# Late modulation rows: the sum over a partition's eight weights moved from TensorE to GpSimd, half of the pieces in the channel stage

## What is computed

```python
c_act = jax.nn.silu(c)                                # 1 x 1024
mod = c_act @ w_ada[l] + b_ada[l]                     # 1 x 6144
sh1, sc1, g1, sh2, sc2, g2 = jnp.split(mod, 6, axis=-1)
u = layernorm(x) * (1 + sc1) + sh1
y = mixer(u, ...)          # mLSTM heads and latent attention heads
x = post_ln(alpha * x + (1 + g1) * y)
u = layernorm(x) * (1 + sc2) + sh2
y = hier_moe(u, ...)
x = post_ln(alpha * x + (1 + g2) * y)

# mLSTM part of the mixer, for each direction, over chunks of 128 tokens
w = exp(d_log - m_t)
s = (q @ k.T) * w
h = (a * (q @ C) + s @ v) / max(|den|, exp(-m_t))
C = decay * C + (k * wg).T @ v
```

## Time and profile before

| what | us |
|---|---|
| three runs: median, lowest, highest | 1534.51, 1533.08, 1534.63 |
| the profiled execution's own time | 1535.46 |
| its span, first to last instruction | 1533.5 |
| TensorE busy | 1487.1 (97%) |
| VectorE busy | 565.2 (37%) |
| ScalarE busy | 357.5 (23%) |
| GpSimd busy | 97.5 (6%) |

### The profile page before, as it was taken

How to read it: one execution, slowest core, us unless ns; L and a number is a source line. 1 busy time by engine, 2 the same in 40 slices (tenths; PEclk the granted TensorE clock), 3 DMA queues, 4 the chain that set the end, 5 groups by cost and what they waited for, 6 DMA issues and landing times. The chain is left out here.

```text
span 1533.5 us, 19984 instructions
## 1 busy us (share of the span) xinstructions
PE 1487.1 (97%) x7403; PEld 818.7 (53%) x7404; DVE 565.2 (37%) x1134; ACT 357.5 (23%) x738; POOL 97.5 (6%) x97
## 2 busy tenths in 40 slices
PE   7999999999989999999999899999999999999997
PEld 4555554447868666674555554444444444444443
DVE  2222126567769433334867711111011011011118
ACT  1122122137624344352111010110111111111111
POOL 0000002000000000000000011111111111111110
PEclk9999999999999999999999899999999999999999
DMA  9401011128730200004111589869789879999965
GB/s 343 159 28 41 0 8 31 41 69 248 248 114 2 110 0 0 0 0 154 76 56 55 192 344 391 370 243 415 317 327 425 314 314 414 423 385 399 425 282 208
DMA packets 101798, 305.51 MB, mean 199 GB/s; under 512 B 18353, under 2 KB 61661, under 8 KB 92536
## 3 DMA queue, kind: packets, MB, share of 16 engines
q1 hardware_dynamic: 93064, 287.08, 48.6%
q0 software_dynamic: 8064, 16.80, 3.0%
q10 hardware_dynamic: 624, 1.03, 0.2%
HBM read 289.86 MB, written 25.76 MB: 206 GB/s over the span
## 5 line engine op out<-in xcount | busy, mean ns | idle before, releaser
L1908 PE MATMUL ps<-w_down_sb,hidT 128*128 x320 | 153.4, 612 | 0.0
L457 PE MATMUL ps<-w_in_tok,uT 128*128 128x512 f32 (+2 forms) x384 | 141.5, 529 | 0.0
L1892 PE MATMUL ps<-w_gate_sb,x_slotsT 128*128 x320 | 140.7, 593 | 0.7 <-ACT x_slotsT L1991 0.7
L1892 PE MATMUL ps<-w_up_sb,x_slotsT 128*128 x320 | 140.6, 592 | 0.0
L1563 PE MATMUL ps<-uT,hT 128*128 128x512 f32 x256 | 112.8, 594 | 0.0
L624 PE MATMUL ps<-uT,mod 128*128 128x512 f32 x256 | 111.0, 594 | 0.8 <-PEq L213 0.8
L2145 DVE TENSOR_TENSOR hid<-silu_g,ps 128x512 f32<-128x512 f32 x20 | 13.8, 688 | 258.0 <-PE ps L1892 258.0
L457 PEld LDWEIGHTS ps<-w_in_tok,uT 128*128 128x128 f32 x384 | 72.7, 190 | 65.3 <-issue 43.9
L1892 PEld LDWEIGHTS ps<-w_gate_sb,x_slotsT 128*128 128x128 f32 x320 | 60.8, 190 | 76.8 <-issue 76.8
L1892 PEld LDWEIGHTS ps<-w_up_sb,x_slotsT 128*128 128x128 f32 x320 | 60.9, 190 | 76.5 <-issue 76.5
L1908 PEld LDWEIGHTS ps<-w_down_sb,hidT 128*128 128x128 f32 x320 | 55.9, 189 | 65.1 <-issue 64.3
(11 more groups left out here) (405 smaller groups left out, 1926.7 us busy)
## 6 DMA issues: line engine op xcount, KB each, us to landing
light_gate_sb<-in_w_gate SPq DMA_DIRECT2D x20, 2048.0 KB
light_up_sb<-in_w_up SPq DMA_DIRECT2D x20, 2048.0 KB
light_down_sb<-in_w_down SPq DMA_DIRECT2D x20, 2048.0 KB
w_gate_sb<-in_w_gate SPq DMA_DIRECT2D x12, 2048.0 KB
w_up_sb<-in_w_up SPq DMA_DIRECT2D x12, 2048.0 KB
w_down_sb<-in_w_down SPq DMA_DIRECT2D x12, 2048.0 KB, 23.1
mod<-in_w_ada SPq DMA_DIRECT2D x8, 1024.0 KB, 8.1
w_ada_late<-in_w_ada SPq DMA_DIRECT2D x8, 1024.0 KB, 6.8
```

The lines of the kernel that those rows point to most:

```text
L457: mm = nc.tensor.matmul(ps[:, 2 + g, 0:n], self.uT[:, k, t * P:(t + 1) * P], wt[:, k, c0:c0 + n], start=k == 0, stop=k == KD - 1)
L1892: m = m_.matmul(ps[:, bank, :], xT[:, k, :], wt[:, bass.ds(buf, 1), k, :].rearrange("p a f -> p (a f)"), start=k == 0, stop=k == KD - 1)
L1908: m = m_.matmul(ps[:, 5 + half, :], hT[:, k, :], wd[:, bass.ds(buf, 1), k, half * 512:half * 512 + 512].rearrange("p a f -> p (a f)"), sta ...
```

## The change

TensorE's `partial(n)`, ScalarE's copy of the partial sums and the tile `late_partial` go. In their place GpSimd runs `late_part` on each piece: one multiplication of 2048 elements to a partition by `c_act`, and three additions of 1024, 512 and 256 elements, which leave one row of 256 in `late_parts`, eight rows long. `spread(n)` reads that row with a matrix of ones in place of `C_SUM`. Pieces 0 to 7 are done by GpSimd in the channel stage (`AHEAD`), behind the gain; they are loaded into `mod[:, 0:2]` and into `qkT[:, 6:8]`, which is free there until ScalarE writes tile 6. Pieces 8 to 15 are done in the mLSTM stage, each once step n-8 has spread its row. The loads are issued in between the others of SyncE, and those of the mLSTM stage wait for `late_part_summed` now.

```diff
+AHEAD = 8
+LATE_HOME = (0, 1, 0, 1, 0, 1, 0, 0, 0, 1, 0, 1, 0, 1, 0, 1)
...
+                modulation(0, 0)
                 weights(2)
+                modulation(1, 0)
                 weights(3)
+                modulation(2, 1)
+                modulation(3, 2)
                 sp.wait_ge(s_atc, 2)
...
                 weights(4)
+                modulation(4, 3)
                 weights(5)
+                modulation(5, 4)
...
                 weights(6)
+                modulation(6, 5)
                 weights(7)
+                modulation(7, 7)
...
-                sp.dma_start(self.w_late0, w_ada[:, :, EARLY * 512:EARLY * 512 + PC]).then_inc(self.s_lw[0], 16)
+                modulation(8, 8)
...
                 pool.wait_ge(s_gm, 1)
+                ch = Chain(pool, s_lsum)
+                for n in range(AHEAD):
+                    self.late_part(pool, ch, n, w_late[LATE_HOME[n]])
+                    pool.wait_ge(self.s_lpart, n + 1)
...
+                    if c == 6:
+                        act.wait_ge(self.s_lpart, 6)
                     a.activation(self.qkT[:, c, :], acc[:, j, :], ACT.Silu).then_inc(s_act[j], 1)
...
+    def late_part(self, pool, ch, n, w):
+        g = self.nc.gpsimd
+        pool.wait_ge(self.s_lw[LATE_HOME[n]], 16 * LATE_HOME[:n + 1].count(LATE_HOME[n]))
+        ch.link(g.tensor_tensor(w, w, self.ca[:].unsqueeze(2).to_broadcast([P, KD, PC]), ALU.mult))
+        ch.link(g.tensor_tensor(w[:, 0:4, :], w[:, 0:4, :], w[:, 4:8, :], ALU.add))
+        ch.link(g.tensor_tensor(w[:, 0:2, :], w[:, 0:2, :], w[:, 2:4, :], ALU.add))
+        g.tensor_tensor(self.late_parts[:, n % AHEAD, :], w[:, 0, :], w[:, 1, :], ALU.add).then_inc(self.s_lpart, 1)
...
                 for k in range(len(HALVES) - 2):
-                    modulation(k + 2)
                     if k + 6 < len(HALVES):
                         maxima(*HALVES[k + 6])
+                    if k % 2 == 0 and 2 <= k <= 12:
+                        modulation(AHEAD + 1 + k // 2)
...
+            @block.gpsimd
+            def _(pool):
+                ch = Chain(pool, s_lsum)
+                for n in range(AHEAD, len(HALVES)):
+                    pool.wait_ge(s_ls, n - AHEAD + 1)
+                    self.late_part(pool, ch, n, w_late[LATE_HOME[n]])
...
-                    act.wait_ge(s_lp, k + 1)
-                    if k > 0:
-                        act.wait_ge(s_ls, k)
-                    a.copy(part[:], ps[:, 7, 0:PC]).then_inc(s_lpc, 1)
...
-                    for k in range(KD):
-                        j = 32 * (k % 4)
-                        m = t.matmul(ps[j:j + 32, 7, 0:PC], self.ca[:, k:k + 1].to_broadcast([P, 32]), w_late[n % 2][:, k, :], start=k < 4, stop=k >= 4)
-                    m.then_inc(s_lp, 1)
...
-                    t.matmul(ps[:, 7, PC:2 * PC], self.c(C_SUM), part[:], start=True, stop=True).then_inc(s_ls, 1)
+                    t.matmul(ps[:, 7, PC:2 * PC], self.c(C_ONE), self.late_parts[:, n % AHEAD, :], start=True, stop=True).then_inc(s_ls, 1)
...
-                    if k > 0:
-                        partial(k)
```

More of the change, by code:

```diff
@@ L528, in project_channels @@
         self.s_lw = [self.sem(f"w_ada_late_loaded{j}") for j in range(2)]
-        self.w_late0 = self.mod[:, 0:2, :].rearrange("p a (k n) -> p (a k) n", n=PC)
+        self.s_lpart = self.sem("late_part_summed")
+        s_lsum = self.sem("late_channel_sums")
+        pieces = lambda ap: ap.rearrange("p a (k n) -> p (a k) n", n=PC)
+        self.w_late0 = pieces(self.mod[:, 0:2, :])
+        self.late_parts = self.sb("late_parts", [P, AHEAD, PC], ctx=up)
+        w_late = [self.w_late0, pieces(self.qkT[:, 6:8, :])]
         w_ada = self.i["w_ada"].rearrange("(p k) n -> p k n", k=KD)
@@ L578, in weights, with modulation @@
                     sp.dma_start(w[:, c % 2], w_q[:, :, c * P:(c + 1) * P]).then_inc(s_w[c % 2], 16)
+                def modulation(n, free):
+                    if free:
+                        sp.wait_ge(self.s_lpart, free)
+                    at = EARLY * 512 + n * PC
+                    sp.dma_start(w_late[LATE_HOME[n]], w_ada[:, :, at:at + PC]).then_inc(self.s_lw[LATE_HOME[n]], 16)
+                modulation(0, 0)
                 weights(2)
+                modulation(1, 0)
                 weights(3)
+                modulation(2, 1)
+                modulation(3, 2)
                 sp.wait_ge(s_atc, 2)
@@ L824, in mlstm @@
         s_lb = [self.sem(f"b_ada_late_loaded{r}") for r in range(4)]
-        s_lp, s_lpc, s_ls, s_late = (self.sem(n) for n in ("late_partial", "late_partial_copied", "late_spread", "late_ready"))
+        s_lsum, s_ls, s_late = (self.sem(n) for n in ("late_sums", "late_spread", "late_ready"))
+        s_lpart = self.s_lpart
         w_ada = self.i["w_ada"].rearrange("(p k) n -> p k n", k=KD)
@@ L838, in mlstm @@
             w_late = [self.w_late0, sb("w_ada_late", [P, KD, PC])[:]]
-            part = sb("late_partial", [P, PC])
             late_rows = [self.mod[:, 2, :], self.mod[:, 3, :], self.mod[:, 4, :], self.gate2[:]]
@@ L849, in modulation @@
                 def modulation(n):
-                    if n > 1:
-                        sp.wait_ge(s_lp, n - 1)
+                    if n > AHEAD + 1:
+                        sp.wait_ge(s_lpart, n - 1)
                     at = EARLY * 512 + n * PC
-                    sp.dma_start(w_late[n % 2], w_ada[:, :, at:at + PC]).then_inc(s_lw[n % 2], 16)
+                    sp.dma_start(w_late[LATE_HOME[n]], w_ada[:, :, at:at + PC]).then_inc(s_lw[LATE_HOME[n]], 16)
                 def maxima(i, d):
@@ L867, in _ @@
                 bias(0)
-                modulation(1)
+                modulation(AHEAD + 1)
                 maxima(*HALVES[4])
@@ L879, in _ @@
                     sp.dma_start(self.lat_g[:, QL // P:], self.i["kv_norm_g"].rearrange("(k p) -> p k", p=P)).then_inc(self.s_gg[1], 16)
-                sp.wait_ge(s_lp, len(HALVES) - 1)
+                sp.wait_ge(s_lpart, len(HALVES) - 1)
                 sp.dma_start(self.wkv, self.i["w_ukv"].rearrange("(k p) n -> p k n", p=P)).then_inc(self.s_wkv, 16)
+            @block.gpsimd
[4 more added lines that the diff above has]
+                    self.late_part(pool, ch, n, w_late[LATE_HOME[n]])
             @block.scalar
@@ L974, in memory, with spread @@
                     m.then_inc(S["cm"][d], 1)
-                def partial(n):
-                    pe.wait_ge(s_lw[n % 2], 16 * (n // 2 + 1))
+                def spread(n):
+                    pe.wait_ge(s_lpart, n + 1)
                     if n > 0:
                         pe.wait_ge(s_late, n)
-                    for k in range(KD):
-                        j = 32 * (k % 4)
-                        m = t.matmul(ps[j:j + 32, 7, 0:PC], self.ca[:, k:k + 1].to_broadcast([P, 32]), w_late[n % 2][:, k, :], start=k < 4, stop=k >= 4)
-                    m.then_inc(s_lp, 1)
-                def spread(n):
-                    pe.wait_ge(s_lpc, n + 1)
-                    t.matmul(ps[:, 7, PC:2 * PC], self.c(C_SUM), part[:], start=True, stop=True).then_inc(s_ls, 1)
+                    t.matmul(ps[:, 7, PC:2 * PC], self.c(C_ONE), self.late_parts[:, n % AHEAD, :], start=True, stop=True).then_inc(s_ls, 1)
                 scores(0, 0)
@@ L991, in _ @@
                 scores(0, 1)
-                partial(0)
                 key_turns(0, 1)
```

## The result

| kernel | device time, us: median (lowest to highest, runs) | ratio to before [95% interval] |
|---|---|---|
| before | 1534.57 (1533.08 to 1535.36, 4) | |
| after | 1574.89 (1572.92 to 1576.98, 4) | 1.0264 [1.0251, 1.0278] |

The change makes the kernel 40 us slower; 58.5 had been forecast. The profiled execution of after took 1576.98 us with a span of 1575.1, 41.6 more than the span of before. To see where that lies I cut both traces at the same three instructions: VectorE's clearing of `qk_raw` (start of the channel stage), its first `W` (start of the mLSTM stage) and its first `lat_tile` (start of the latent attention).

A forecast was written before the change was run, and what follows sets the result against it. TensorE was taken to bound both stages, VectorE close behind in mLSTM steps; 1535.46 + 37 (channel) + 21 (mLSTM) = 1593.5, less 0.95 to the median, say 1593 us. Own range 1570 to 1608, 1618 with clock; 8 in 10: 1521 to 1618.

The forecast's parts named there:

- The choice: Both stages: VectorE instructions with two SBUF tensors and GpSimd's instructions exclude each other, each waiting out the other's; chance 0.57.
- Channel stage, TensorE's wait: Ahead of the sums by head, 15 VectorE instructions each wait 2.15 us for GpSimd, 32 us less 5: some 27 us.
- Channel stage, the rest: Behind the sums by head, convolutions, scans and the last tile's halves are drawn out by GpSimd's instructions: 10 us more.
- The lower bound of the sum: Channel stage: VectorE's 58 us plus GpSimd's 69 one after the other, against 101.7 available: at least 26 us longer.
- mLSTM stage, the products: Removing eight products saves TensorE 1.00 us a step, 5.63 to 4.63, just above VectorE's 4.54: 15 us.
- mLSTM stage, the waits: VectorE's L1026 and L1016 wait for GpSimd some 4.5 us a piece: 36 us, less 15 for products gives +21.
- The sign named: mLSTM stage: if the forecast is right, L1016's counterpart shows single durations near 4.8 us.
- The clock: Nothing added; each long wait can cost some 2 us of slower products behind it, ten of them 20 us.
- (1): Only VectorE's one-input fast kinds (TENSOR_SCALAR, SBUF copies) exclude GpSimd, two-tensor instructions don't: 1527 us; chance 0.24.
- (2): VectorE's chained instructions keep GpSimd off until VectorE is idle: +26 and +9 us, 1570 us; chance 0.11.
- (3): Nothing excludes, and the 4.07 us TENSOR_SCALAR had another cause: -13, 1521 us; chance 0.04.
- (4): The exclusion is partial, so the 15 us gain and the waits cancel: near 1534 us; chance 0.04.

The follow-up runs named there:

- sums_left_out: After, with GpSimd's multiplication and three additions of each piece left out, only clearing the rows: channel stage 122.04 us, mLSTM stage 79.39 (totals not comparable).
- write_only: After, with GpSimd's four instructions a piece replaced by clearings that read nothing: channel stage 125.21 us, mLSTM stage 86.92 (totals not comparable).
- short_multiplications: After, with GpSimd's multiplication of 2048 elements split into four of 512: 1552.92 us, 1.0125 of before.
- start_after_sums: After, with GpSimd's first piece started only behind VectorE's sums by head and SyncE's loads later to match: 1563.82 us, 1.0186 of before.

## Why the prediction was right, and where it was not

**The choice was right.** Two-tensor instructions in SBUF are held until GpSimd's instruction in flight is over, GpSimd's next waits for them in turn, and those with one tensor in PSUM are not held (691 ns). This was the step on which the sign hung, and sums_left_out, write_only and short_multiplications show it from three sides. The forecast had the two stages in the right order: +37 and +21, measured +27.7 and +14.0. Both are too high, by 9 and 7 us. The reason given for the choice was only half right, though: it took the two-tensor instructions to be like the held TENSOR_SCALAR, and in write_only the two part ways, 1285 ns unchanged for the one and 812 to 1442 for the other.

**Channel stage, TensorE's wait: 27 forecast, 21.9 measured.** VectorE's way from L751 to the end of the copy took 33.1 us (240.41 to 273.51) instead of 12.6: 20.5 us of holds. The gain came 2.0 us later (231.50 instead of 229.50 us), and TensorE got there 0.6 us later: 20.5 + 2.0 - 0.6 = 21.9. The sum had 15 hand-overs of 2.15 us less 5. Measured were 13 instructions of GpSimd, with 27.4 us of its own time, of which 6.9 lay beside VectorE's waits and its free instructions. The mis-sized terms are GpSimd's work in this stretch (32 us for 27.4) and what lies beside it (5 for 6.9); the late gain was not in the sum. The multiplication was estimated from the gain, 4.48 us, and takes 3.60; the additions (2.34, 1.27, 0.72) were estimated well.

**Channel stage, the rest: +10 forecast, +5.8 measured.** The lower bound of the sum had VectorE's 58 us and GpSimd's work one after the other; with the shorter multiplication it becomes 58 + 8 x 7.93 - 101.7 = 20 us, and the stage is only 8 us above it, though GpSimd waited 34.5 us for loads into `mod` and 2.5 for one into `qkT`. (With the prediction's own terms the bound is 58 + 69 - 101.7 = 25.3 us, not 26; its upper bound of +44 follows from no sum that it shows, 9 us a piece adding 3 us to the work.) Its waits from 220 to 370 us, in total, and in the timeline the longest of them:

```profile
POOL mod L847 <- DMA mod<-in_w_ada: 34.5, 4, 19.7
```

```profile
298.86 3.60 POOL L847 TENSOR_TENSOR mod<-mod,c_act 128x2048 f32<-128x2048 f32 x1 [19.65 <-DMA mod<-in_w_ada]
```

That load stands in SyncE's list behind the store of the sums, which left at 283.34 us instead of 258.73 because the sums were late. The prediction costed SyncE's waits at nothing, and for TensorE that was so in after, but they took GpSimd out of the middle of the stage and left VectorE alone for that long. The prediction followed each queue for what it delays and not for what it relieves. On TensorE's side 3.9 of the +5.8 are the wait at the barrier (5.87 us ahead of the first mLSTM product instead of 1.97), and 1.4 are slower products (the four tiles from 274.09 us take 56.48 us instead of 55.10). The 0.92 of the stage's clock is mostly that of the long wait: 0.84 up to 273.5 us, 0.97 behind it.

**mLSTM stage, the products: 15 forecast, 20.6 measured.** The step was to fall from 5.63 to 4.63 us and fell from 5.64 to 4.44, both from start to start. So a piece of eight products was worth 1.20 us of TensorE's list and not the 1.00 between the start of the products and the next weight load: with them gone the output products ahead take 0.10 us less, start to start, and the state's products behind 0.09 less. 15 x 1.20 = 18.0 us. VectorE's list is close behind, as forecast, but was put too high, at 4.54 us: it takes 4.37, and with 4.54 the step could not have come down to 4.44. The remaining 2.6 us are won mostly in the first two steps, where in before TensorE also waits 3.4 us for ScalarE's copy; the prediction had put the copies at nothing for the steady part only.

**mLSTM stage, the waits: 36 forecast, 34.7 measured** (114.06 - 79.39), 4.3 a piece for 4.5. But they lie elsewhere than forecast. The sign named was a counterpart of L1016 near 4.8 us, held by a multiplication; L1045 never takes more than 2.51 us, because the first addition holds it, and the multiplication falls on the scaling of `q`, 2.4 us a piece on average. The prediction had each case (1.96 us for the addition, up to 3.5 for the multiplication), but not that all eight pieces would fall into this one. The long steps, forecast near 10 us, took 8.3 to 9.3. The twin of after in start_after_sums took 5.7 us less with the same code, so the agreement to 1.3 us is partly luck: what a piece costs depends on where in the step it begins.

**The clock** was left at nothing, with up to 10 us of the range for it. After's stage has 0.88 granted. TensorE's output products from 380 to 402 us take 312 ns on average there and 275 in before and in sums_left_out. This slowing is inside the 34.7 us; no run separates it from the waits, but the 33.5 us of holds in VectorE's durations leave 1.2 us for it and all else.

**The rivals.** (1) is refuted for sums that read and is what write_only does. (2), VectorE keeping GpSimd off, is refuted: the timeline shows them taking turns, one for one. (3) and (4) are refuted by the same rows and by the time. The mark set for rival 1, long durations at the TENSOR_SCALARs and copies alone, told the two apart as it was meant to.

## What to carry to other kernels

Work for an idle GpSimd isn't free when it reads SBUF: ask which of VectorE's instructions read two tensors there, and whether somebody waits for VectorE. Here such work paid only in stretches where VectorE is idle, and the budget can be counted beforehand: with 8 us a piece, five pieces made this kernel 6 us faster, six 1.5 us (within what can be told from nothing), eight and eight made it 40 us slower. Where it must lie beside VectorE's work, cut GpSimd's instructions short, since each held instruction waits for the end of the one in flight.

## What the runs showed of the hardware that I had not expected

- The hold is in the duration of the held instruction and not in its idle time. A copy of 64 elements of 3.63 us, or a mean of 1859 ns where single ones take 680, is its sign; the views of waits name nobody.
- An instruction of GpSimd that only writes holds TENSOR_SCALARs (812 to 1442 ns) but not two-tensor instructions (1285 and 682 ns, as when GpSimd is idle).
- GpSimd's multiplication of 2048 elements by a broadcast column takes 3.60 us, 1.76 ns an element, while the gain with 4096 takes 8.85, 2.16 ns an element, and the addition of 1024 takes 2.34, 2.29 ns.
- The same code of the mLSTM stage took 114.06 and 108.39 us; 4.9 of the 5.7 us are shorter holds of one instruction, as GpSimd and VectorE met in another phase.
- A hold can also lengthen GpSimd's own instruction: beside VectorE's two scans of 2.3 us an addition of 512 elements that takes 1.27 us alone took 3.90 (after, 319.77 us).
